# Attention's sums of values: one f32 product per key tile, or three f32r products of high and low parts

## What is computed

```
def _attend(q, k, v, scale):
    s = jnp.einsum('bqkgd,bskd->bkgqs', q, k).astype(jnp.float32) * scale
    p = jax.nn.softmax(s, axis=-1).astype(v.dtype)
    return jnp.einsum('bkgqs,bskd->bqkgd', p, v)
```

## Time and profile before

| | us |
|---|---|
| median of 3 runs | 5835.86 (5834.09 to 5843.02) |
| the profiled execution | 5834.1 |
| its span, first to last instruction | 5832.8 |
| projections stage in it | about 1025 to 1487 |
| attention stage in it | about 1487 to 2718 |

### The profile page before, as it was taken

How to read it: one execution, slowest core, us unless ns; L and a number is a source line. 1 busy time by engine, 2 the same in 40 slices (tenths; PEclk the granted TensorE clock), 3 DMA queues, 4 the chain that set the end, 5 groups by cost and what they waited for, 6 DMA issues and landing times. The chain is left out here.

```text
span 5832.8 us, 89498 instructions
## 1 busy us (share of the span) xinstructions
PE 5492.7 (94%) x29296; PEld 4644.4 (80%) x29297; DVE 3485.0 (60%) x6477; ACT 2399.0 (41%) x4640; POOL 817.7 (14%) x611
## 2 busy tenths in 40 slices
PE   8999988888899999998969999999999999999993
PEld 7777767777677777775758999999999888899893
DVE  6666757323455566665774745655656645467767
ACT  3444421333333334443333533443445534356654
POOL 1101125223000000000540100110101100010113
PEclk9999989999899999999989999999999999999997
DMA  3333244344411001101423744545556635467666
GB/s 139 116 116 109 76 148 139 118 115 124 133 50 51 35 30 37 60 8 67 151 92 125 241 133 159 183 155 162 197 177 225 232 120 166 129 221 240 238 219 226
DMA packets 244895, 796.24 MB, mean 137 GB/s; under 512 B 21472, under 2 KB 155232, under 8 KB 208224
## 3 DMA queue, kind: packets, MB, share of 16 engines
q1 hardware_dynamic: 214832, 704.37, 34.5%
q0 software_dynamic: 27536, 84.88, 6.6%
q10 hardware_dynamic: 2336, 4.45, 0.2%
HBM read 656.50 MB, written 137.13 MB: 136 GB/s over the span
## 5 line engine op out<-in xcount | busy, mean ns | idle before, releaser
L2686 DVE TENSOR_TENSOR e_wl<-r_raw,e_wh 128x1024 fp32r<-128x1024 f32 x770 | 930.5, 1222 | 517.8 <-DVEq L2315 517.4
L2602 ACT CAST e_wh<-r_raw 128x1024 fp32r (+1 forms) x770 | 790.2, 1042 | 1058.7 <-ACTq L2315 1058.6
L2535 PE MATMUL ps<-e_hT,e_wl 128*128 128x192 f32 (+4 forms) x4096 | 1219.8, 298 | 0.0
L2530 PE MATMUL ps<-e_hT,e_wh 128*128 128x256 f32 (+3 forms) x2816 | 900.8, 320 | 9.3 <-PEq L2315 9.2
L2534 PE MATMUL ps<-e_hT,e_wh 128*128 128x256 f32 (+3 forms) x2816 | 899.8, 320 | 0.0
L2535 PEld LDWEIGHTS ps<-e_hT,e_wl 128*128 128x128 f32 x4096 | 774.5, 189 | 16.5
L2530 PEld LDWEIGHTS ps<-e_hT,e_wh 128*128 128x128 f32 x2816 | 530.1, 188 | 28.7 <-issue 11.5
L1710 PE MATMUL ps<-a_PT,a_V 128*128 128x512 f32 (+1 forms) x1088 | 548.9, 596 | 0.7 <-ACT a_oT L1766 0.7
L2534 PEld LDWEIGHTS ps<-e_hT,e_wh 128*128 128x128 f32 x2816 | 530.0, 188 | 16.4
L2556 PE MATMUL ps<-e_wh,e_aTh 128*128 128x512 f32 x1248 | 511.6, 410 | 4.9 <-PEq L2315 4.9
L1779 DVE TENSOR_REDUCE a_sc<-ps 128x1 f32<-128x416 f32 (+1 forms) x640 | 364.8, 588 | 253.1 <-PE ps L1688 253.1
(11 more groups left out here) (367 smaller groups left out, 9195.2 us busy)
## 6 DMA issues: line engine op xcount, KB each, us to landing
r_raw<-in_wgu SPq DMA_DIRECT2D x130, 2048.0 KB, 7.9
r_raw<-in_wdn SPq DMA_DIRECT2D x64, 2048.0 KB, 7.7
m_raw<-in_w SPq DMA_DIRECT2D x56, 1024.0 KB, 4.9
qTd<-p_qt SPq DMA_DIRECT2D x32, 640.0 KB, 6.5
e_bd<-in_bdn SPq DMA_DIRECT2D x32, 512.0 KB, 3.7
kTd<-p_kt SPq DMA_DIRECT2D x32, 448.0 KB, 3.7
a_Q<-qTd SPq DMA_DIRECT2D x7, 2048.0 KB, 8.5
a_K<-kTd SPq DMA_DIRECT2D x5, 2064.0 KB, 17.0
```

Of the source, the lines that this page charges most:

```text
L2530: t = pe.matmul(p[:, 0:v], wh, E.hT[:, 0, k, 0:v], start=(k == 0), stop=False)
L2535: t = pe.matmul(p[:, 0:v], wl, E.hT[:, 0, k, 0:v], start=False, stop=(k == 7))
L2602: act.copy(E.wh[:, h, x], raw[:, 2048 * h + 1024 * i:2048 * h + 1024 * i + 1024]).then_inc(E.hi_full, 1)
L2686: return dve.tensor_tensor(lo, src, hi.bitcast(F32), ALU.subtract)
```

## The change

- **Projections.** ACT's copies of values round to f32r (the high part). DVE gets two more subtractions per tile: `vlg` (256 columns) ahead of its step ("z", n, 2), and `vln` (512 columns) after ("kn", n). SP stores high and low parts with three DMAs in place of one; `vd` is twice as large.
- **Values products.** `PT` has a high and a low part, of 256 columns (two query tiles). Key tile j has three f32r products of 256 columns per pair of query tiles. `value_tiles` spreads the 17 tiles of a pair over two steps from m = 2G + 3 (nine in odd steps, eight in even), 0, 3, 2, 2 and 2 of them after the five transposed groups.
- **High and low of the probabilities.** ACT now copies all five transposed groups (high part, step "th"), interleaved with the exponentials by the list `by_turns`; DVE subtracts all five (low part) after ACT's copy. PE may refill bank 5 or 6 only after DVE's subtraction. ACT's copy of finished sums moves to the start of step m = 4G + 7.
- **Loads of values.** One set in place of two (each twice as large), in four portions; PE reports tiles 3, 7 and 11 of the last pair of a head (`vfree`), and SP loads each portion when it is free, the fourth when the head's last sums are complete. These loads now stand after the store of group 4h + 2 and ahead of the loads of queries and keys for head h + 2.

The core of the diff:

```diff
@@ projections
-        sp.wait_ge(*P.a.at("vn", n))
-        sp.dma_start(P.vd[:, 0:r, t, :].rearrange("h p d -> p h d"), P.vt[0:r]).then_inc(*P.vtst.more())
+        sp.wait_ge(*P.v.at("vn", n))
+        for hs, z, x in ((slice(0, 6), 0, P.vt), (slice(0, 4), 1, P.vln.rearrange("p (a b) -> p a b", a=4)),
+                         (slice(4, 6), 1, P.vlg.rearrange("p (a b) -> p a b", a=2))):
+            sp.dma_start(P.vd[hs, 0:r, t, z, :].rearrange("h p d -> p h d"), x[0:r].bitcast(F32)).then_inc(*P.vtst.more())
...
         if n:
-            act.wait_ge(P.vtst.sem, 16 * n)
+            act.wait_ge(P.vtst.sem, 48 * n)
...
+        if n:
+            dve.wait_ge(P.vtst.sem, 48 * n)
+        low(P.vlg[0:r], bank("z", n, 2)[0:r, 256:512], P.vt[0:r, 4:6, :].rearrange("p a b -> p (a b)"))
         dve.tensor_tensor(xg[:, 4:6, :], bank("z", n, 2)[0:r, 0:256].rearrange("p (h w) -> p h w", h=2),
...
+        dve.wait_ge(*a.at("vnh", n))
+        low(P.vln[0:r], bank("vn", n)[0:r, :], P.vt[0:r, 0:4, :].rearrange("p a b -> p (a b)")).then_inc(*v.step("vn", n))
@@ attention: buffers, order
-            self.V = sb("V", [128, 2, NT, 128])
+            self.V = sb("V", [128, NT, 2, 128], F32R)
...
-    P.PT = sb("PT", [128, 2, NT, 512])
+    P.PT = sb("PT", [128, 2, 2, NT, 256], F32R)
...
+def by_turns(m):
+
+    th, s = [("th", m - 1, c) for c in range(5)], [("s", m, c) for c in range(5)]
+    return [th[0], th[1], s[0], th[2], s[1], th[3], s[2], th[4], s[3], s[4]]
...
 def value_tiles(m):
 
-    if m < 5:
+    if m < 3:
         return None, []
-    G, z = (m - 5) // 4, (m - 5) % 4
-    return G, list(range(4 * z, 4 * z + 4)) + ([16] if z == 3 else [])
+    return (m - 3) // 2, list(range(0, 9) if m % 2 else range(9, NT))
+
+
+
+V_PARTS = ((0, 4), (4, 8), (8, 12), (12, NT))
@@ attention: SP
     def values(h):
         n = key_slot(h)
-        b = n % 2
-        sp.dma_start(P.V[0:NM, b, 16, :], vd[n, 0:NM, 16, :]).then_inc(*P.vld[b].more())
-        sp.dma_start(P.V[:, b, 0:16, :], vd[n, :, 0:16, :]).then_inc(*P.vld[b].more())
+        for i, (lo, hi) in enumerate(V_PARTS):
+            if n and i < 3:
+                sp.wait_ge(P.vfree, 3 * (n - 1) + i + 1)
+            if n and i == 3:
+                sp.wait_ge(*filled(P, ("o", 4 * (h - 1) + 3)))
+            sp.dma_start(P.V[:, lo:min(hi, 16)].bitcast(F32), vd[n, :, lo:min(hi, 16)]).then_inc(*P.vld[i].more())
+            if hi == NT:
+                sp.dma_start(P.V[0:NM, 16].bitcast(F32), vd[n, 0:NM, 16]).then_inc(*P.vld[i].more())
...
+        if i == 8 and h + 1 < 8 and key_slot(h + 1) != key_slot(h):
+            values(h + 1)
         if i == 8 and h + 2 < 8:
             load(h + 2)
@@ attention: PE
-        t = pe.matmul(ps[b][:, :], P.V[0:r, n % 2, j, :], P.PT[0:r, G % 2, j, :], start=(j == 0), stop=(j == NT - 1))
-        if j == NT - 1:
+            pe.wait_ge(*v.at("t", 2 * G + 1, 4))
+        if first_pair(G) and j == V_PARTS[part][0]:
+            pe.wait_ge(P.vld[part].sem, (32 if part == 3 else 16) * (n + 1))
+        b, _, _ = P.bank[("o", G // 2)]
+        for k, (x, y) in enumerate(((0, 0), (0, 1), (1, 0))):
+            t = pe.matmul(ps[b][:, 256 * half:256 * half + 256], P.V[0:r, j, x, :], P.PT[0:r, G % 2, y, j, :],
+                          start=(j == k == 0), stop=(j == NT - 1 and k == 2))
+        if j == NT - 1 and half:
             t.then_inc(P.full[b], 1)
+        elif last_pair(G) and j in (3, 7, 11):
+            t.then_inc(P.vfree, 1)
@@ attention: DVE
-            for c in range(1, 5):
-                dve.wait_ge(*filled(P, ("t", n, c)))
...
+            for c in range(5):
+                dve.wait_ge(*a.at("th", n, c))
...
+                dve.tensor_tensor(lo, src, hi.bitcast(F32), ALU.subtract).then_inc(*v.step("t", n, c))
```

More of the change, by code:

```diff
@@ L1347, in project_act @@
         p = product("vn", n)
[L1348 removed]
+        act.copy(P.vt[0:r, 0:4, :].rearrange("p a b -> p (a b)"), p[0:r, :]).then_inc(*a.step("vnh", n))
         if whole:
@@ L1559, in attend_stage @@
         back = m >= 9 and m % 4 == 1 and m // 4 - 2 < N // 4
+        out = m >= 7 and m % 4 == 3 and (m - 7) // 4 < N // 4
+        if out:
+            o += [("o", (m - 7) // 4)]
+            a += [("o", (m - 7) // 4)]
         if turned:
             t += [("t", m - 1, c) for c in range(5)]
[L1562 to L1566, removed]
+            v += [("t", m - 1, c) for c in range(5)]
             v += [("sum", m - 1), ("rec", m - 1)]
+        a += [k for k in by_turns(m) if (turned if k[0] == "th" else m < N)]
         if back:
@@ L1640, in attend_sync @@
         h, i = G // 4, 4 * (G % 4)
-        if i == 0 and 2 <= h + 1 < 8 and h + 1 not in (5, 7):
-            load_values(h + 1)
         sp.wait_ge(*P.v.at("u", G))
@@ L1725, in attend_pe @@
         G, tiles = value_tiles(m)
-        tiles = iter(tiles if G is not None and G < P.N // 4 else [])
+        tiles = iter(tiles if G is not None and G < P.N // 2 else [])
         for c in range(5):
@@ L1741, in attend_act @@
     for m in range(P.N + 6):
[L1742 to L1762 removed]
+        if m >= 7 and m % 4 == 3 and (m - 7) // 4 < P.N // 4:
+            G = (m - 7) // 4
             act.wait_ge(*filled(P, ("o", G)))
@@ L1766, in attend_act @@
             act.copy(P.oT[:], ps[P.bank[("o", G)][0]][:, :]).then_inc(*a.step("o", G))
+        for what, n, c in by_turns(m):
+            if what == "th" and 0 <= n < P.N:
+                act.wait_ge(*filled(P, ("t", n, c)))
+                p = ps[P.bank[("t", n, c)][0]]
+                q = slice(n % 2 * 128, n % 2 * 128 + 128)
+                if c < 4:
+                    act.copy(P.PT[:, n // 2 % 2, 0, 4 * c:4 * c + 4, q],
+                             p[:, :].rearrange("p (k q) -> p k q", k=4)).then_inc(*a.step("th", n, c))
+                else:
+                    act.copy(P.PT[0:NM, n // 2 % 2, 0, 16, q], p[0:NM, 0:128]).then_inc(*a.step("th", n, c))
+            if what == "s" and n < P.N:
+                if c == 0:
+                    act.wait_ge(*v.at("shift", n))
+                    if n >= 2:
+                        act.wait_ge(*filled(P, ("t", n - 2, 4)))
+                        act.wait_ge(*v.at("sum", n - 2))
+                lo, w = SCW[c]
+                p = ps[P.bank[("s", n, c)][0]]
+                act.activation(P.P[:, n % 2, lo:lo + w], p[:, 0:w], ACT.Exp, bias=P.sc[:, n % 2, 6:7],
+                               scale=SQK_M if P.steps[n][0] < 4 else SQK_G,
+                               accum_out=P.sc[:, n % 2, 8 + c:9 + c]).then_inc(*a.step("s", n, c))
 def attend_dve(nc, P):
```

77 lines of the change are left out of this document (23 added, 54 removed).

## The result

The changed kernel takes **5797.7 us** (median of 4 runs, 5794.2 to 5799.6), the kernel before beside it 5835.6 (4 runs). The ratio is 0.9933, with a 95% interval of 0.9921 to 0.9945: 38 us less. The direction was right and the time lies in the range (5760 to 5802), but the gain is 38 us where 56 were forecast, and 5797.7 lies outside the forecast's own range (5768 to 5792). The profiled execution took 5799.55, the slowest of its four; that of before, 5834.09, was the fastest of its four.

What follows compares the result with a forecast made beforehand. Attention was taken as bound by a dense stream of PE instructions, their number times the distance between starts. Terms -79.4, +11.8, +7.7, +1 and +3 summed to -55.9 us, giving 5780 us, range 5760 to 5802.

Steps and rivals of the forecast that it cites:

- the forecast's own range (5768 to 5792): Whole kernel: range of the main forecast without its rivals, 0.003 us per product and half the wait; chance 0.62.
- The values products (-79.4): Attention on PE: 1088 records at 0.430 us become 3264 products at 0.119 us, -79.4 us.
- The rival of weight loads that are not hidden: Values products: each of 3264 weight loads costs 0.19 us, +620 us, 6400 us in all; chance 0.05.
- The tile of 16 rows (+11.8): Values products, pair's end: going from 128 rows to 16 and back costs 0.37 us, 32 more times, +11.8 us.
- The turning of banks (+7.7): Attention, banks 5 and 6: PE waits 0.06 us for DVE's subtraction in each of 128 steps, +7.7 us.
- T + 2.00: Attention step: earliest start of the third transposed group, 2.00 us after T, the start of the transposes.
- The rival with this name: Turning of banks binds: DVE 0.3 us later in each of 128 steps, 38 us, 5818 us; chance 0.08.
- The start of head 0 (+1): Steps 1 and 2 of head 0, without values products to hide DVE's work: about 1.3 us per step show, net +1 us.
- The end (+3): End of attention: last store issued sooner but queued behind the next stage's loads, +3 us (0 to 4).
- The loads of values (0): Attention, change of heads: later loads of values cost nothing, with 0 to 20 us as the upper side.
- The projections (0): Projections stage: added DVE subtractions and SP DMAs fit into slack, 0 us; 19 us if both lie on the loop.
- a neighbour pays: Rival: projections (19 us) or the reload of values (20 us) show, 5799 or 5800 us; chance 0.14.

Runs made afterwards that it cites:

- wide rows: Changed kernel with the last key tile computed as 128 rows, rows 16 to 127 zeroed, in place of 16 rows: 5780.5 us, attention 1153.8 against 1178.1.
- two tiles ahead: Changed kernel with two value tiles in place of three ahead of the third transposed group: 5837.7 us, ratio to before 0.9999.
- the second comparison: The changed kernel run again, unmodified, against the kernel before beside it: 5801.1 us against 5840.8.

## Why the prediction was right, and where it was not

**The values products (-79.4): right.** 0.12 us each in place, from two independent places (six against four products; twelve in 1.50 us). The Trainium skill, "TensorE: Matmul & The Clock Gate", section "Back-to-back issue gap", has 109 ns for an isolated matmul of this width; the traces bear the experts' rows out and not this figure for products that follow each other with a weight load each. The rival of weight loads that are not hidden is refuted, since 3264 of them follow at 0.12, and with it, for this stream, the rule of the same page's "What overlaps and what doesn't". That rival's price of 0.19 us per load came from the tile of 16 rows, and went away there with as many loads in place. What I hadn't seen: the first product of a group now starts 0.03 us after the last transpose and not 0.11, and the second product 0.20 us after the first and not 0.12. Eight transposes with what follows therefore read as 0.79 us where the earlier trace rows have 0.87, but from transpose to transpose it is still 0.109, and the group as a whole costs the same.

**The tile of 16 rows (+11.8): right** for the order of the changed kernel, and the experiment with wide rows shows the cause: 24.3 us for 64 pairs, 0.38 each. In another order it is less, as said above.

**The turning of banks (+7.7): mechanism right, size too small.** T + 2.00 came out exactly. The failed step is "It waits 0.06 us in each of 128 steps: +7.7": behind the wait PE needs 0.05 to 0.06 us more for its next group. The heads show it, 160.1 and 130.3 us against 159.2 and 129.2 by the forecast (4 x 39.8, 4 x 32.3), about 1 us per head, 8 us over eight. The rival with this name (DVE late by 0.3 us) didn't come about, but its warning holds: with two tiles ahead the chain cost 41 us.

**The start of head 0 (+1): failed.** "About 1.3 us per step show" was right for the turned groups (4.1 us against 2.8). The working behind the net does not come out as written (twice 1.3 against "about 1 us each of steps 2 to 4" is less than nothing); from the traces, two steps with some 2.3 us of waits replace four with some 0.9, which is +1. But I left out what the waits of PE do to its clock. The scores behind them took 6.3 us and not 4.7, twice; filling the waits gave 3.0 us back. 8 and 3 are the 11 us that attention misses.

**The end (+3): right.** 4.44 us from the last store but one to the last (4.4), 3.6 us lost behind the loads, 3.3 of them won back by queuing the loads one store earlier.

**The loads of values (0): right.** PE waits nowhere for `a_V`.

**The projections (0): open.** The stage took 464.7 us against 461.7. It was 460.6 to 471.1 us (mean 466.3) in the eleven profiled executions with the new projections, and 461.7 and 464.9 in two with the old; single tiles jitter by 1.5 us in both. In the last tile of the changed kernel the store of `vt` is issued 5 us later than before, since it waits for DVE's subtraction, and the first scores of attention come 2.4 us later. That store is not what holds the stage's end: the barrier opens 9.4 us after PE's last product in both. The medians point to a small cost. For each of the eleven I compared the gain over before beside it with what its attention and its tail explain; the gain falls short by -1 to 10 us, 5 in the mean. Two or three of them may be the projections. No run separated them.

**The sum.** By the parts as measured, attention gives 48.1 and the tail takes 3.6: 44.5 us, of which the medians show 38 and, in the second comparison, 39.7. Of the 18 us between 56 and 38, then, 11 are the two steps above and the rest lies outside attention, unsettled. So the range held partly by luck: 5797.7 lies where the rival "a neighbour pays" (5799 or 5800) had put it, but the loads of values never made PE wait and the projections are open; what is shown to have cost time is the restart and the clock, which I hadn't foreseen.

## What to carry to other kernels

When a product gets cheaper, work out the chain of banks behind it as a time of its own (here 2.00 us for a bank through PE, ACT, DVE and back) and put just enough work ahead of the wait; one key tile per step in the wrong place took the whole gain. A wait of PE costs more than its length: some 0.06 us to start again, and in a stretch where little else runs the clock as well, so look at the granted clock of the stretch behind it. And before any of that, look for a tile of another shape in the stream: 16 rows in place of 128 cost 24 us, and the fill of zeros that took them away is two clears of 1.3 us in all on POOL, at the start. And when two edits touch the same stretch, don't add up their gains: here 31 us became 25.

## What the runs showed of the hardware

- Going from products with 128 rows to three with 16 and back costs 0.38 us where the three stand behind a transpose and ahead of the scores (0.25 to 0.29 where they stand ahead of the last transpose), though the 16 rows do less work.
- Two waits of 0.96 and 0.81 us within 4.1 us, in which PE was busy for 2.33, were followed by a stretch at the 1.2 GHz level (mean clock 0.73 over 6.3 us; 0.52 in 3.5 us of it); with PE busy for 3.89 of 4.0 us it stayed at 2.4 GHz. Before the change, with waits of 0.24 us in these places, the granted clock was 1.00 too.
- Of the same four transposes, those behind a wait of PE take 0.41 us to the next products and those without 0.36; the second transpose follows the first after 0.164 us and not 0.109.
- Products of 256 columns (f32r), each with its own weights of 128 columns, follow each other at 0.119 to 0.12 us; two PE records of an f32 product of 512 columns take 0.86.
